# Input by features, parameters as columns and weights stored tile by tile, laid out by the host, in a two-layer decoder trunk

## The reference

```
def reference(x, positions, norm_mix, norm_ffn, norm_final, conv_w_in, ..., ffn_w_down):
    for i in range(DEPTH):                        # DEPTH 2, x is (1, 256, 2048)
        h = rms_norm(x, norm_mix[i])
        if i % N_MIXERS == 0:
            mix = conformer_conv(h, ...)          # layer 0
        else:
            mix = diff_attention(h, positions, ...)   # layer 1
        x = x + mix
        h = rms_norm(x, norm_ffn[i])
        x = x + conv_ffn(h, ...)                  # D_FF 5504
    return rms_norm(x, norm_final)

def conformer_conv(x, w_in, b_in, dw, dw_b, ln_g, ln_b, w_out, b_out):
    h = x @ w_in + b_in                           # 2048 -> 4096
    a, gate = jnp.split(h, 2, axis=-1)
    h = a * jax.nn.sigmoid(gate)
    h = causal_dwconv(h, dw, dw_b)                # 31 taps
    h = jax.nn.silu(layer_norm(h, ln_g, ln_b))
    return h @ w_out + b_out
```

## Time and profile before

| | |
|---|---|
| time, median of 3 runs | 2141.56 us (2141.47 to 2142.43) |
| time of the profiled execution | 2142.64 us |
| its span | 2140.8 us |
| PE busy | 2125.7 us (99%), granted clock 0.999 on the mean |
| DVE, ACT busy | 68%, 49% |
| DMA moved | 399.07 MB, 186 GB/s on the mean |

### The profile page before, as it was taken

One profiled execution on the slowest core, in us unless ns is written; L12 is line 12 of the kernel. 1 busy time (PEld: TensorE's weight loads), 2 busy tenths in 40 slices (PEclk: granted clock), 3 DMA queues, 4 the chain that ended last, 5 costly groups with the idle time before them and its releaser, 6 DMA issues.

```text
span 2140.8 us, 30475 instructions
## 1 busy us (share of the span) xinstructions
PE 2125.7 (99%) x11011; PEld 1812.3 (85%) x11011; DVE 1452.6 (68%) x2137; ACT 1056.8 (49%) x1501; POOL 45.7 (2%) x50
## 2 busy tenths in 40 slices
PE   9999999999999999999999999999999999999998
PEld 7788788888888888888888888888888888888887
DVE  6766757777777774454688867667777777764444
ACT  7554655544445443444554444554544445444443
POOL 5300000000000000000000000000000000000000
PEclk9999999999999999999999999999999999999999
DMA  8555456666666655555656554566666666656553
GB/s 309 175 186 191 138 178 183 190 191 183 194 184 189 191 185 189 193 190 191 191 163 176 181 175 155 191 182 183 190 190 184 194 183 189 192 190 215 195 195 114
DMA packets 513820, 399.07 MB, mean 186 GB/s; under 512 B 6558, under 2 KB 425848, under 8 KB 513408
## 3 DMA queue, kind: packets, MB, share of 16 engines
q1 hardware_dynamic: 513568, 397.96, 60.0%
q10 hardware_dynamic: 192, 0.28, 0.0%
HBM read 396.11 MB, written 2.10 MB: 186 GB/s over the span
## 4 chain that ended last, share of the span: by engine, by line
PE 95%; DVE 2%; DMA 1%; ACT 1%; SPq 0%; issue 0%; DVEq 0%; ACTq 0%
PE acc L1520 35%; PE acc L1525 18%; PE acc L1554 12%; PE acc L1555 12%; PE acc L1556 12%; PE acc L1826 1%; PE acc L1825 1%; PE acc L1824 1%; DMA sb_stage<-in_conv_w_in 1%; DVE sb_w_lo L918 1%; PE aux L1595 0%; PE aux L1835 0%; ACT sb_w_hi L564 0%; PE aux L1783 0%; PE aux L1664 0%
## 5 line engine op out<-in xcount | busy, mean ns | idle before, releaser
L918 DVE TENSOR_TENSOR sb_w_lo<-sb_stage,sb_w_hi 128x1024 fp32r<-128x1024 f32 (+1 forms) x743 | 904.9, 1221 | 516.8 <-ACT sb_w_hi L564 513.4
L564 ACT ACTIVATE sb_w_hi<-sb_stage 128x1024 fp32r<-128x1024 f32 (+1 forms) x743 | 780.4, 1053 | 657.4 <-PE acc L1556 373.9
L1520 PE MATMUL acc<-sb_normed,sb_w_hi 128*128 128x512 f32 x3264 | 1027.6, 396 | 0.0
L1525 PEld LDWEIGHTS acc<-sb_normed,sb_w_lo 128*128 128x128 f32 x3264 | 613.2, 188 | 144.8
L1525 PE MATMUL acc<-sb_normed,sb_w_lo 128*128 128x256 f32 x3264 | 641.4, 278 | 0.0
L1520 PEld LDWEIGHTS acc<-sb_normed,sb_w_hi 128*128 128x128 f32 x3264 | 497.7, 189 | 0.6
L1554 PE MATMUL acc<-sb_w_hi,sb_hidden 128*128 128x512 f32 x674 | 262.5, 389 | 0.0
L1556 PE MATMUL acc<-sb_w_hi,sb_hidden 128*128 128x512 f32 x674 | 262.3, 389 | 0.0
L1555 PE MATMUL acc<-sb_w_lo,sb_hidden 128*128 128x512 f32 x674 | 262.3, 389 | 0.0
L576 ACT ACTIVATE sb_corr<-acc 128x256 f32<-128x256 f32 x204 | 76.8, 376 | 210.8 <-PE acc L1525 210.7
L1556 PEld LDWEIGHTS acc<-sb_w_hi,sb_hidden 128*128 128x128 f32 x674 | 126.5, 188 | 26.4
(11 more groups left out here) (221 smaller groups left out, 1645.1 us busy)
## 6 DMA issues: line engine op xcount, KB each, us to landing
sb_stage<-in_ffn_w_gate SPq DMA_DIRECT2D x86, 1024.0 KB, 5.4
sb_stage<-in_ffn_w_up SPq DMA_DIRECT2D x86, 1024.0 KB, 5.5
sb_stage<-in_ffn_w_down SPq DMA_DIRECT2D x80, 1024.0 KB, 5.0
sb_stage<-in_attn_w_qkv SPq DMA_DIRECT2D x48, 1024.0 KB, 5.3
sb_stage<-in_conv_w_in SPq DMA_DIRECT2D x30, 1024.0 KB, 5.6
sb_stage<-in_conv_w_out SPq DMA_DIRECT2D x16, 1024.0 KB, 5.1
sb_stage<-in_attn_w_o SPq DMA_DIRECT2D x16, 1024.0 KB, 5.0
sb_stage<-in_ffn_w_down SPq DMA_DIRECT2D x8, 768.0 KB, 4.4
```

The lines of the kernel that those rows point to most:

```text
L564: nc.scalar.activation(w_hi[:, (2 * first + h) % PIECES, 0:size], stage[:, first % STAGES, off:off + size], ACT.Copy).then_inc(hi_ready, 1)
L918: nc.vector.tensor_tensor(w_lo[:, slot, 0:size], stage[:, first % STAGES, off:off + size], w_hi[:, slot, 0:size].bitcast(F32), ALU.subtrac ...
L1520: nc.tensor.matmul(acc[:, bank, :], w_hi[:, slot, q * P:(q + 1) * P], operand[:, k, :], start=begin, stop=False, skip_group_check=True)
L1525: return nc.tensor.matmul(acc[:, bank, T:2 * T], w_lo[:, slot, q * P:(q + 1) * P], operand[:, k, 0:T], start=False, stop=end, skip_group_c ...
```

## The change

The host now writes the arrays in the order in which the kernel loads them:

- All weights lie tile by tile: for each column chunk, 128 partitions, and on each the tiles of the contraction one behind the other. What a load of a block writes to one partition is one contiguous run of 8 KB, where it was four runs of 2 KB (wide blocks) or sixteen of 512 B (gate, up, query and key weights).
- x comes twice: by features (`x_cols`) straight into `x_t`, which lies in the memory of `conv`, and later by tokens into `resid`, two loads of 1 MiB, for the squares and the residual.
- Parameters come as columns straight into `par_d`, `par_c` and `par_f`. `turn_x`, `turn_params`, the first turn, and `keep_params` are gone; `scale_subln` keeps one multiply of the latter. `keep_clock` at the start goes from 5 and 6 calls to 5 and 13.
- Jobs move between the iterations of ACT and DVE, as shown below the diff.

```diff
             def load_x(begin, end):
-                return sp.dma_start(resid[:, :, begin:end], x_in[0].rearrange("(b p) d -> p b d", p=P)[:, :, begin:end])
+                return sp.dma_start(x_t[:, begin:end, :], x_cols[:, begin:end, :])
...
             conv_in_block(STAGES)
-            sp.dma_start(rope_c[:, :], rope_rows).then_inc(rope_loaded, 16)
-            sp.dma_start(pos_i[:, :], positions[0:1, :].to_broadcast([ROT, T])).then_inc(rope_loaded, 16)
-            sp.dma_start(rows_n[:, :], norm_ffn.rearrange("l (c p) -> (l c) p", p=P)).then_inc(par_c_loaded, 16)
+            for b in range(TB):
+                sp.dma_start(resid[:, b, :], x_in[0][b * P:(b + 1) * P, :]).then_inc(resid_loaded, 16)
+            conv_in_block(STAGES + 1)
             sp.dma_start(dft_in[:, :, :], dft_rows).then_inc(dft_loaded, 16)
             sp.dma_start(rows_t[:, :], conv_dw).then_inc(taps_loaded, 16)
             load_in_rows(0)
-            for at in range(STAGES + 1, 2 * STAGES):
+            for at in range(STAGES + 2, 2 * STAGES):
                 conv_in_block(at)
...
             def x_hi(q, part=range(4)):
+                act.wait_ge(x_first if q == 0 and part[0] < 2 else x_loaded[q], 16)
                 for k in [4 * q + f for f in part]:
-                    act.wait_ge(x_turned, k + 1)
-                    operand(0, normed[:, k, 0:T], aux[:, k % BANKS, 0:T], par_d[:, k:k + 1], 0)
+                    operand(0, normed[:, k, 0:T], x_t[:, k, :], par_d[:, k:k + 1], 0)
...
                 hi(0, (0, at + 2), 0)
-                if at in (2, 3):
-                    x_squares(2 * (at - 2))
-                    x_squares(2 * (at - 2) + 1)
-                if at == X_PARTS:
+                if at in (4, 5):
+                    hi(0, (0, at + 2), 1)
+                if at in (3, 4):
+                    x_squares(2 * (at - 3))
+                    x_squares(2 * (at - 3) + 1)
+                if at == 4:
                     taps_hi()
+                if at == 5:
                     rms_root(STAT["input"])
-                if j == 4:
+                if j == (4 if c else 5):
                     open_gate(c)
...
-            pe.wait_ge(par_d_loaded, 16)
-            nc.tensor.transpose(acc[:, 0, 0:2 * KD], rows_d[:, :], ident[0:2 * KD, 0:2 * KD]).then_inc(par_turned, 1)
-            turn_x(0, [0, 1])
-            keep_clock(acc[:, 3, 0:P], 6)
-            pe.wait_ge(par_kept, 1)
+            keep_clock(acc[:, 3, 0:P], 13)
...
+    arrays["in_x_cols"] = np.ascontiguousarray(tokens.T.reshape(-1, P, tokens.shape[0]).transpose(1, 0, 2))
+    def tiles(w, width):
+        w = w.reshape(*w.shape[:-2], -1, P, w.shape[-1] // width, width)
+        return np.ascontiguousarray(np.moveaxis(w, (-2, -3, -4), (-4, -3, -2)))
```

More of the change, by code:

```diff
@@ L393, in conv_in_block @@
                 c, j = ORDER["conv_in"][at]
-                first = WIDE * (c // 2) + (0 if c % 2 else D)
+                unit = c // 2 + (0 if c % 2 else CH)
                 if at >= STAGES:
@@ L1107, in _ @@
                         measure_conv(c - 1, b)
+                if at not in (4, 5):
+                    lo(0, (0, at + 2), 1)
                 if at == 8:
-                    keep_params()
-                lo(0, (0, at + 2), 1)
+                    scale_subln()
                 if at < 2:
@@ L1614, in stat @@
                 ins.then_inc(stat_ready, 1)
-            def turn_rows(bank, at, src, rows):
-                return nc.tensor.transpose(aux[:, bank, at:at + rows], src, ident[0:rows, 0:rows])
             def keep_clock(out, count):
@@ L1626, in _ @@
             keep_clock(acc[:, 3, 0:P], 5)
-            def turn_x(q, part=range(4)):
-                pe.wait_ge(x_first if q == 0 and 0 in part else x_loaded[q], 16)
-                for k in [4 * q + f for f in part]:
-                    if q:
-                        pe.wait_ge(operand_ready, OPER["x"] + k + 1 - BANKS)
-                    for b in range(TB):
-                        ins = nc.tensor.transpose(aux[:, k % BANKS, b * P:(b + 1) * P], resid[:, b, k * P:(k + 1) * P],
-                                                  ident[:, :])
-                    ins.then_inc(x_turned, 1)
             def turn_taps(n):
@@ L1906, with columns @@
     arrays["in_dft_rows"] = transform_rows(inputs["conv_dw"].shape[1])
+    def columns(v):
+        return np.ascontiguousarray(v.reshape(-1, P).T)
+    for name in ("norm_mix", "norm_ffn", "conv_ln_g", "conv_ln_b", "attn_subln_g"):
+        arrays[f"in_{name}"] = columns(inputs[name])
+    for name in ("ffn_dw", "ffn_dw_b"):
+        v = inputs[name]
+        arrays[f"in_{name}"] = columns(v).reshape(P, *v.shape[:-1], -1)
+    tokens = inputs["x"][0]
+    arrays["in_x_cols"] = np.ascontiguousarray(tokens.T.reshape(-1, P, tokens.shape[0]).transpose(1, 0, 2))
+    def tiles(w, width):
+        w = w.reshape(*w.shape[:-2], -1, P, w.shape[-1] // width, width)
+        return np.ascontiguousarray(np.moveaxis(w, (-2, -3, -4), (-4, -3, -2)))
+    qkv = inputs["attn_w_qkv"][0]
+    values = qkv.shape[1] // 3 * 2
+    arrays["in_attn_w_qkv"], arrays["in_attn_w_v"] = tiles(qkv[:, 0:values], P), tiles(qkv[:, values:], 4 * P)
+    for name in ("conv_w_in", "conv_w_out", "attn_w_o"):
+        arrays[f"in_{name}"] = tiles(inputs[name][0], 4 * P)
+    arrays["in_ffn_w_down"] = tiles(inputs["ffn_w_down"], 4 * P)
+    for name in ("ffn_w_gate", "ffn_w_up"):
+        arrays[f"in_{name}"] = tiles(inputs[name], P)
     args = [nc.dram_tensor(k, a.shape, mybir.dt.from_np(a.dtype), kind="ExternalInput").ap()
```

129 lines of the change are left out of this document (52 added, 77 removed).

## The result

The change made the kernel slower by 2.85 us on the medians of 19 runs each: 2145.28 us (2144.42 to 2146.71) against 2142.43 us (2141.15 to 2143.42), ratio 1.0014, 95% interval 1.0008 to 1.0020. That is within the 0.2% for which the prediction had its largest chance, and inside its range. The forecast was 2.6 us slower. Its absolute time, 2144.2 us, is 1.1 us low mainly because it starts from the median of three runs, 2141.56 us; 19 runs of the kernel before have 2142.43. The profiled execution took 2146.71 us with a span of 2144.9, the longest of the 19.

What follows compares the result with a forecast made beforehand. PE, busy 99% of the span, bounds the kernel; only the first 75 us, with scarce DMA, can move. Landing 39.5, 10.25 to the taps, 27.9 to `forward` give 77.7 against 75.15: 2141.56 + 2.6 = 2144.2 us, range 2139 to 2149.

Steps and rivals of the forecast that it cites:

- The forecast, 2.6 us slower: Whole kernel: `forward` starts at 77.7 us against 75.15, so the time is 2144.2 us; chance of +1 to +5 us 0.54.
- The layout of the weights brings nothing from 75 us on: From 75 us on: PE waits for no load there, so the weights' layout can bring nothing.
- PE's 5 us are not gained: First stage: of PE's removed 5.0 us, 2.2 would be in hand at block 6's second half, then PE waits for the taps.
- PE starts 1 to 3 us later: Start: 36 rows of `keep_clock` end at 8.5 to 10.7 us, where the first weight product started at 7.67; hidden later.
- Block 6 lands at 39.5 us: First-stage loads: 33.2 + 7.4 - 0.6 - 0.5 gives block 6's landing, bounds 38.3 and 40.9 us.
- 10.25 us from there to the taps: Block 6's landing to taps ready at 49.75 us: two `w_hi`, four squares, ACT's taps, DVE's share.
- 27.9 us from the taps to `forward`: ACT's and DVE's work on blocks 7 to 10, transform, lambda and `glu`, between taps and `forward`; bounds 26.5 and 30.8 us.
- PE stands at the taps at 45.1 us and waits 4.6: Block 6's second half: PE arrives at 45.1 us and waits 4.6 us for the taps instead of 1.5.
- A wait of 3.5 us for `tap_rows` at block 8: Ahead of block 8's second half: PE arrives at 61.9 us, the last bank is emptied at 65.4 us.
- the fourth rival: Clock falls in PE's new wait, costing 1.6 us, covered by the wait at block 8; uncovered +4.2 us; chance 0.08.
- The rival of slow long runs: First-stage loads: 8 KB runs read at 303 GB/s, block 6 lands at 48.5 us, time 2153; chance 0.13.
- The rival of the taps not waited for: First stage: taps ready by 45.1 us, `forward` at 69.1, 6 us sooner, time 2135.5; chance 0.08.

Runs made afterwards that it cites:

- e12: The changed kernel with 19 calls of `keep_clock` between the halves of block 2, as much PE work as the removed turns of x; 2145.36 us, ratio 1.0016.
- e3: The changed kernel with 22 more calls of `keep_clock` on PE ahead of its wait for the taps; 2145.09 us, ratio 1.0013.
- e4: The changed kernel with all weights in the old layout (runs of 2 KB and 512 B); 2145.86 us, ratio 1.0017.
- e8: The changed kernel with the taps padded by the host to 128 rows of 8 KB, to all 128 partitions; 2144.40 us, ratio 1.0009.
- e7: The changed kernel with the first biases loaded behind block 6 instead of ahead of it; 2143.86 us, ratio 1.0008.
- e6: The changed kernel with block 6 loaded ahead of the transform, the taps and the first biases, no job moved; 2139.80 us, ratio 0.9989.
- e11: The kernel before the change with the exponential for lambda behind block 9's second half and DVE's small sums behind it; 2140.37 us, ratio 0.9994.
- e1: The changed kernel with the taps split by ACT and DVE right behind block 5, in the wait for block 6; 2140.34 us, ratio 0.9992.
- e2: The changed kernel with all of ACT's and DVE's odd jobs (squares, taps, root, gate) in or right behind the waits for blocks 5 and 6; 2140.41 us.
- e5: The kernel of e2 with the exponential for lambda behind block 9's second half and DVE's two small sums behind it; 2139.49 us, ratio 0.9986.
- e9: The kernel of e5 with the memset of `prod` done by POOL at its start instead of by DVE; 2137.04 us, ratio 0.9977.
- e10: The kernel of e9 plus the 128 tap rows of e8 and the gate's sigmoid behind block 7's `w_hi`; 2136.74 us, ratio 0.9974.

## Where the prediction was right, and where not

The chain is best checked with all profiled executions side by side (us; the column of block 6 has the start of its first `w_hi`, taps the first turned taps on PE, the last column the median of all runs):

| kernel | block 6 | taps | forward | span | median |
|---|---|---|---|---|---|
| before | 37.02 | 48.88 | 75.15 | 2140.8 | 2142.4 |
| the change | 40.79 | 50.89 | 79.19 | 2144.9 | 2145.3 |
| e12 PE's work back | 39.96 | 50.11 | 78.42 | 2143.1 | 2145.4 |
| e3 clock kept up | 39.19 | 49.25 | 77.65 | 2142.3 | 2145.1 |
| e4 old rows | 40.22 | 50.18 | 78.57 | 2144.3 | 2145.9 |
| e8 taps in 128 rows | 39.28 | 49.41 | 77.70 | 2143.6 | 2144.4 |
| e7 biases later | 38.79 | 48.97 | 77.36 | 2142.1 | 2143.9 |
| e6 block 6 first | 35.63 | 45.59 | 73.62 | 2138.2 | 2139.8 |
| e11 before, exponential later | 37.39 | 49.34 | 75.62 | 2140.2 | 2140.4 |
| e1 taps early | 39.79 | 45.53 | 73.75 | 2139.3 | 2140.3 |
| e2 all jobs early | 40.21 | 45.95 | 73.58 | 2138.2 | 2140.4 |
| e5 exponential later | 39.90 | 45.62 | 71.75 | 2137.7 | 2139.5 |
| e9 memset on POOL | 39.57 | 45.34 | 69.47 | 2135.4 | 2137.0 |
| e10 all of it | 39.16 | 45.09 | 68.91 | 2133.9 | 2136.7 |

- **The forecast, 2.6 us slower: right.** Measured 2.85 us on the medians. The profiled executions lie 4.1 us apart (spans 2144.9 and 2140.8), since that of the change was 1.4 us above its median. By the terms below the chain is some 0.7 us longer than I had it, 0.4 at the landing and 0.3 behind it.
- **The layout of the weights brings nothing from 75 us on: right.** From `forward` to the end it is 2064.6 to 2066.0 us in every kernel, e4 with the old rows among them.
- **PE's 5 us are not gained: right,** and shown by e12.
- **PE starts 1 to 3 us later: wrong in the profile after.** From 1.70 to 5.36 us PE did 17 rows in 3.66 us, from 5.36 to 7.50 us 22 in 2.14 us, twice as fast. The view gives a granted clock of 1.00 for both, so that it was the clock is read from the rates. The 36 rows took 6.0 us instead of 7 to 9. In the other executions they took 5.6 to 7.1 us (e4, e8), so the lower end of my range does occur. It changed nothing, since PE waits later anyway.
- **Block 6 lands at 39.5 us (38.3 to 40.9): right.** Executions with the same loads up to it show 39.19, 39.57, 39.79, 39.90, 39.96, 40.21 and 40.79 us. The profiled one of the change is the latest of them, so its `forward` is late too. The rates were near mine: 428 GB/s from 10 to 20 us where I had 423, 348 at the start where half of the way from 318 to 408 is 363. The mean of the seven is 39.9 us.
- **10.25 us from there to the taps: right;** in the seven kernels of the table from the change to e6 it is 10.0 to 10.2. DVE's taps took 2.28 us here and 2.79 in e11; before 2.72.
- **27.9 us from the taps to `forward`: right in its sum,** 28.3 to 28.4 in the six kernels from the change to e7, 28.0 in e6. From block 6 to `forward` it is 38.3 to 38.6 us in the six, 38.0 in e6, where I had 38.15.
- **PE stands at the taps at 45.1 us and waits 4.6: the wait right, the time not quite.** It stood there at 46.17 us and waited 4.72. PE lost 1.49 us ahead of block 6's first half, where I had no wait, and the taps were late by the same landing.
- **A wait of 3.5 us for `tap_rows` at block 8: wrong in the profile after.** There is none: PE lost those 3 us to the low clock instead (13 products in the 5.67 us that it was busy, where full clock does 25). This was the mechanism of the fourth rival, and as that rival said, the wait at block 8 covers it: e3 keeps the clock up and gets the waits, 1.9 us of them, and the same time. The size of the wait was off too: PE got there 0.5 us later than 61.9 (62.35 in e3), and in e3 the last two turns started 14.8 us behind the taps (64.04 less 49.25), where I had the last at 15.6.
- **The rival of slow long runs: fallen.** Blocks now lie 32 KiB apart from partition to partition and read at 419 to 428 GB/s. The Trainium skill (DMA: Bandwidth & Descriptors, "Latency and other measured facts") has figures for copies between tensors in HBM whose rows on the partitions lie a large power of two apart: 207 GB/s at 512 KiB and 103 at 4 MiB, where 214 is its full rate. So the halving is at 4 MiB, and 512 KiB costs next to nothing. No run here has rows so far apart. What I had put forward for this rival, the slow stretch of the taps, is real, but by e8 it is their 96 partitions and not their 8 KB.
- **The rival of the taps not waited for: possible, as e1 shows, but not with this order.** My price for it, 2135.5 us, took for granted that nothing follows. To come to 2136.74 it took the moves of e2, e5, e8 and e9 as well. The exponential and the memset gave 0.9 and 2.45 us; whether they need e2's moves wasn't run. One argument against this rival didn't hold: 30.7 us from 2 us on end at 32.7, which is ahead of the 34.9 that it asks for.
- **Sums.** 24 products of 0.225 us are 5.40 us, not 5.45. The trace has their starts 0.227 apart, which gives the 5.45; the 222 take in products that only overlap the ends of the stretch. The terms from the landing to the taps, as written, add up to 10.1 us and not 10.25, and 77.65 less 75.15 is 2.5 and not 2.6. None of them moves the forecast by more than 0.2 us.

What I didn't see: that the change leaves ACT idle for 4.7 us ahead of block 5 and again ahead of block 6, with the taps, whose load had landed by 36.4 us (e1), waiting behind. The order of the jobs costs the change 5 us. Moving the taps alone (e1) brings it to 2.1 us under the kernel before, which is not yet clear of the noise; e5, e6, e9 and e10 are. I had priced this link right as part of a chain, without saying that it was free to go.

The profiled times of single executions lie up to 1.4 us from the median of their kernel, and two things that vary in the traces are of that size: the landing of block 6, over 1.6 us for the same loads, and whether the clock falls at about 220 us, as at 223.02 before and at 227.23 in the change. In seven of the fourteen profiled executions it does, for 3.41 us, and the way from `forward` to the end is 2065.5 to 2066.0 us there, else 2064.6 to 2065.0.

## What to carry to other kernels

When work is taken from the busiest engine, look in each other engine's list for a job that stands behind a wait for a load though its own data is there; such a link holds the end just as firmly as work does, and e12 is the cheap test of it (put the work back and see if the time moves). Move a queue's order before its bytes: one block ahead of four loads (e6) gave 5.5 us, while an eighth less DMA time from the layout (53.1% of the span for 60.5%) gave nothing that could be told from noise (0.6 us on the medians). And a tiny instruction that waits for another engine, like the exponential, belongs behind the long ones that don't.

## What I had not expected of the hardware

- A load of 0.75 MiB in rows of 8 KB to 96 partitions runs slower than one of 1 MiB to 128: 259 against 437 GB/s while it runs, its packets 532 ns on the median against 309, and the stretch behind it suffers with it. Padding it with rows that nobody reads took 0.9 us off the kernel by the medians, less than the intervals tell apart.
- The clock at 0.50 behind PE's wait of 4.7 us lasted 6.83 us, and 22 calls of `keep_clock` in the wait kept it at 1.00. The Trainium skill (TensorE: Matmul & The Clock Gate, "Why this matters for your kernels") advises against idle gaps between bursts; the trace agrees that the clock falls behind one, and shows that keeping it up need not be worth anything.
- POOL clears 128x2048 elements in 1.80 us (the memset in e10), DVE in 1.76. POOL is otherwise idle there, so the move cost nothing: PE starts at 1.67 us with it and without it.
